# Experts stage of a hybrid encoder step: late dense tokens take the gates as stationary operand, and a piece's sum is kept in its PSUM bank by ScalarE and TensorE

## Chip, cores and metric

One core of one Trainium2 chip. The metric is the device time of one launch in microseconds. Every number below is in microseconds unless marked otherwise.

## The reference, cut to what matters

One layer of a streaming encoder for 1024 prompt tokens and 8 x 16 sample tokens (T = 1152 tokens, D = 1024 features) is computed in fp32. Its last part is a product-key expert layer: each token picks 8 x 16 of 128 x 128 experts, and every expert is one row of u and one row of v.

```python
w = jax.nn.softmax(fv, axis=-1)
act = jax.nn.gelu(jnp.einsum("thkd,td->thk", u[eidx], tb).astype(jnp.float32))
return jnp.einsum("thk,thkd->td", (w * act).astype(tb.dtype), v[eidx])
...
x = x + gate2 * peer_ffn(h2, peer_wq, peer_keys, peer_u, peer_v)
```

After that comes the final RMSNorm.

## The kernel before

Stages run one after the other: projections, a state-space scan, attention, branches, picks and gates, and from 2888.9 us to about 4825 us the experts stage (`phase_experts`), then `finish_output`. The diff touches the last two and the allocation of one array.

**Two ways to do the experts at once.** The first TD = 640 tokens ("dense") go through all 16,384 experts on TensorE, with the gates of the picked experts in a dense table and zeros elsewhere. The other 512 tokens (ST = 4 tiles of 128, "sparse") gather only their picked rows of u and v by indirect DMA, 128 rows of 4 KB (512 KB) at a time; VectorE forms the dot products and adds the weighted rows.

**Batches.** There are 64 batches of E = 2 blocks of 128 experts for the dense tokens, and two picks for each of the four sparse tiles. Each batch loads 2 x 512 KB of u, 2 x 512 KB of v, half of a 1280 KB slice of gates, and gathers 16 x 512 KB.

**Dense work of batch b.** fp32 products are made of three fp32r products (hi by hi, hi by lo, lo by hi), so every array is rounded by ScalarE (`round_u`, `round_v`, `round_g`) and its rest is formed by VectorE (`rest_of_u`, `rest_of_v`, `rest_of_g`). TensorE runs ahead with the u products of batch b+1 (L2290: 8 slices x 3 x 2 halves of 320 tokens, for each of 2 blocks = 96 matmuls of 320 columns into `ps`); ScalarE applies gelu into `act_` (L2365), VectorE multiplies by the gates (L2440), and the v products of batch b follow. Those are 8 output blocks d of 128 features, 6 matmuls each over 640 tokens:

- `keep(d)` for d = 0 to 3: v is stationary, and the sums stay in PSUM over all 64 batches, 512 tokens in `kept` (L2302, 24 matmuls of 512 columns in a batch) and 128 tokens in `kept_late` (L2301, 24 matmuls of 128 columns).
- `piece(b, j)` for j = 0 to 7 (SUMS = 8) does d = 4 to 7 in halves of 320 tokens into the one bank `pv` (L2310, 48 matmuls of 320 columns). Before each piece TensorE waits for `sum_r`: VectorE must have added the piece before it to `acc` in SBUF (`add_sums`, L2453). There is no second buffer.

```python
pe.wait_ge(sum_r, b * SUMS + j + START)
...
dve.wait_ge(sum_mm, b * SUMS + j + 1 + START)
v.tensor_tensor(acc[:, j // 2, a:a + HW], acc[:, j // 2, a:a + HW], pv[:, 0:HW], ALU.add).then_inc(sum_r, 1)
```

**Order.** The instruction order of each engine is written out by hand in a function `batch`. TensorE: the u products of block 0 of batch b+1 (48 matmuls), a wait for `v_lo` and `g_lo`, then `keep`, `piece` and two slices of block 1's u products in turn. ScalarE: `round_v` twice (each waits until all pieces of b-1 are done), `round_g`, then for m = 0 to 7 `weigh(b, m)` (gelu of a dot product and its share, two tiny instructions L2381 and L2383) with gelu and the rounding of u and g between them. VectorE: `rest_of_v`, `apply_gate`, `rest_of_v`, `rest_of_g`, then `dots(b, m)` (L2459), `add_rows(b, m)` (L2467) and the eight `add_sums` mixed. `add_rows(b, m)` needs `weigh(b, m)`, which needs `dots(b, m)`.

**Queues.** SP issues the loads of u, v and gates, each when the buffer is free (`u_lo`, `v_lo`, `gated`); u is loaded up to three batches ahead. GpSimd issues the gathers in the order u row 0, v row 0, u row 1, ... into four slots for u and four for v; each waits until VectorE has read the slot (`dot_r`, `row_r`).

**Finish.** ScalarE copies the kept sums to SBUF (L2424, L2425). `finish_output` takes the eight feature blocks in turn: x plus gated sums for the dense tokens (L2563), TensorE transposes the four sparse tiles (L2595), VectorE adds these, then squares, norm and store.

## Time and profile before

| | us |
|---|---|
| median of 3 runs (4875.52 to 4882.52) | 4880.63 |
| profiled execution, its own time | 4877.16 |
| span of its trace | 4875.0 |
| TensorE / VectorE / ScalarE / GpSimd busy, of the span | 4501.8 / 3520.9 / 1814.5 / 1519.1 |
| mean granted share of TensorE's clock | 0.961 |

Spans of instructions overlap where an engine is pipelined, so an engine's time for one instruction is read from the starts of two neighbours, not from the duration. DMA share is what the packets took, as a share of the 16 DMA engines' time; it can pass 1 a little.

### The profile page before, as it was taken

To read this page: it belongs to the slowest core of one execution; us is meant where nothing else is said; L and a number is where in the kernel's file an instruction comes from. 1 tells how busy PE (TensorE), PEld (TensorE's weight loads), DVE (VectorE), ACT (ScalarE), POOL (GpSimd) and SP (SyncE) were. 2 spreads that over 40 slices of the span, in tenths; PEclk is the share of its full clock that TensorE was granted. 3 is DMA by queue.
4 is the path that set the end of the run, shared out by engine and by line. 5 is a ranking of instruction groups with operands and counts; after the bars stand their busy time and mean duration, and the time that the engine had idled before them with its cause. 6 is when DMAs were issued, how large, how long until landed. Compare 5 with 4: busy or idle time off the path is not lost. (4 is left out here: it accounts for less than half of the span.)

```text
span 4875.0 us, 82654 instructions
## 1 busy us (share of the span) xinstructions
PE 4501.8 (92%) x28695; PEld 4177.5 (86%) x28695; DVE 3520.9 (72%) x6718; ACT 1814.5 (37%) x3800; POOL 1519.1 (31%) x1358
## 2 busy tenths in 40 slices
PE   7999999799989899969885779999999999999996
PEld 5999999799976598968874669999999999999995
DVE  3101555476754323447999979999999999999998
ACT  3111333244435531234444963333333333333332
POOL 0000000011210000000000017777777777777773
PEclk8999999899988899989997999999999999999998
DMA  4332222344433244338995569999999999999996
GB/s 164 107 137 96 87 89 84 129 141 142 138 115 62 68 161 168 140 124 306 352 329 199 207 235 367 359 378 372 371 370 375 375 370 362 372 380 377 377 371 247
DMA packets 351143, 1170.28 MB, mean 240 GB/s; under 512 B 40160, under 2 KB 91808, under 8 KB 344608
## 3 DMA queue, kind: packets, MB, share of 16 engines
q0 software_dynamic: 147456, 536.94, 29.3%
q1 hardware_dynamic: 160544, 483.06, 27.7%
q10 hardware_dynamic: 43008, 148.53, 8.1%
q8 instruction: 78, 1.28, 0.1%
q14 instruction: 57, 0.47, 0.0%
HBM read 971.20 MB, written 197.46 MB: 240 GB/s over the span
## 5 line engine op out<-in xcount | busy, mean ns | idle before, releaser
L2280 POOL DMA_INDIRECT ex_vr<-in_expert_v,ex_at x512 | 637.8, 1246 | 231.8 <-issue 154.3
L2278 POOL DMA_INDIRECT ex_ur<-scr_u_rows,ex_at x512 | 569.5, 1112 | 277.2 <-issue 118.1
L2467 DVE SCALAR_TENSOR_TENSOR ex_acc_rows<-ex_vr,ex_wt,ex_acc_rows 128x1024 f32<-128x1024 f32 x512 | 648.9, 1277 | 1.0 <-DMA ex_vr<-in_expert_v,ex_at 0.3
L2459 DVE SCALAR_TENSOR_TENSOR ex_ur<-ex_ur,h_rows 128x1024 f32<-128x1024 f32 x512 | 616.0, 1217 | 32.0 <-DMA ex_ur<-scr_u_rows,ex_at 30.8
L2272 POOL COPY ex_at<-picked_at 128x4 uint32 x128 | 96.5, 754 | 1465.5 <-POOLq L125 1465.0
L990 POOL TENSOR_TENSOR sd_cts<-sd_cT,sd_ea 128x512 f32<-128x512 f32 x72 | 98.6, 1369 | 1261.2 <-ACT sd_ea L880 1261.2
L2290 PE MATMUL ex_ps<-hd_hi,ex_u_hi 128*128 128x320 f32 x2048 | 469.5, 310 | 19.9 <-PEq L125 16.4
L2290 PE MATMUL ex_ps<-hd_lo,ex_u_hi 128*128 128x320 f32 x2048 | 469.3, 311 | 0.0
L2290 PE MATMUL ex_ps<-hd_hi,ex_u_lo 128*128 128x320 f32 x2048 | 468.5, 310 | 0.0
L2381 ACT ACTIVATE ex_gel<-ex_dot 128x1 f32<-128x1 f32 x512 | 103.7, 203 | 897.4 <-DVE ex_ur L2459 897.3
L479 DVE TENSOR_TENSOR pr_w_lo<-pr_w,pr_w_hi 128x1024 fp32r<-128x1024 f32 x56 | 68.6, 1226 | 487.8 <-ACT pr_w_hi L475 487.8
L2290 PEld LDWEIGHTS ex_ps<-hd_hi,ex_u_hi 128*128 128x128 f32 x2048 | 343.6, 189 | 20.6 <-issue 17.7
L2310 PE MATMUL ex_pv<-ex_g_hi,ex_v_hi 128*128 128x320 f32 x1024 | 329.1, 321 | 21.3 <-DVE ex_acc L2453 20.7
L2290 PEld LDWEIGHTS ex_ps<-hd_lo,ex_u_hi 128*128 128x128 f32 x2048 | 344.8, 189 | 0.0
L2290 PEld LDWEIGHTS ex_ps<-hd_hi,ex_u_lo 128*128 128x128 f32 x2048 | 344.1, 189 | 0.0
L331 PE MATMUL pr_ps<-h_hi,pr_w_hi 128*128 128x384 f32 x1392 | 320.7, 338 | 13.1 <-DVE h_lo L304 9.9
L331 PE MATMUL pr_ps<-h_lo,pr_w_hi 128*128 128x384 f32 x1392 | 317.8, 336 | 0.0
L331 PE MATMUL pr_ps<-h_hi,pr_w_lo 128*128 128x384 f32 x1392 | 317.6, 335 | 0.0
L2310 PE MATMUL ex_pv<-ex_g_lo,ex_v_hi 128*128 128x320 f32 x1024 | 316.8, 309 | 0.0
L2310 PE MATMUL ex_pv<-ex_g_hi,ex_v_lo 128*128 128x320 f32 x1024 | 315.3, 308 | 0.0
L331 PEld LDWEIGHTS pr_ps<-h_hi,pr_w_hi 128*128 128x128 f32 x1392 | 248.1, 189 | 18.7 <-issue 15.0
L331 PEld LDWEIGHTS pr_ps<-h_lo,pr_w_hi 128*128 128x128 f32 x1392 | 249.7, 189 | 0.0
(363 smaller groups left out, 11130.1 us busy)
## 6 DMA issues: line engine op xcount, KB each, us to landing
pk_raw_u<-in_expert_u SPq DMA_DIRECT2D x128, 512.0 KB, 6.5
scr_u_rows<-pk_rows_u ACTq DMA_DIRECT2D x128, 512.0 KB, 6.2
ex_u<-in_expert_u SPq DMA_DIRECT2D x128, 512.0 KB, 6.7
ex_v<-in_expert_v SPq DMA_DIRECT2D x128, 512.0 KB, 8.2
scr_gate<-gt_stage SPq DMA_DIRECT2D x10, 4096.0 KB, 12.6
ex_gate<-scr_gate SPq DMA_DIRECT2D x32, 1280.0 KB, 8.8
pr_w<-in_w_main SPq DMA_DIRECT2D x58, 512.0 KB, 4.6
scr_xbc<-pr_out ACTq DMA_DIRECT2D x32, 576.0 KB, 3.8
```

The costliest lines, as they stand in the source:

```text
L331: last = nc.tensor.matmul(ps[:, c, 0:CW], w[a][:, k], x[b][:, k, c * CW:(c + 1) * CW], start=(k == 0 and (a, b) == SPLIT[0]), stop=(k == k ...
L479: nc.vector.tensor_tensor(w2[1][:, s], w[:, s], w2[0][:, s].bitcast(F32), ALU.subtract).then_inc(w_lo[s], 1)
L990: nc.gpsimd.tensor_tensor(cts[:, q], cT[:, s, at].unsqueeze(1).to_broadcast([P, R, P]), ea[:, q], ALU.mult).then_inc(cts_r[q], 1)
L2272: nc.gpsimd.tensor_copy(at_now[:, h], at[:, :, ds(b * 2 + h, 1)].rearrange("p s j -> p (s j)")).then_inc(now_r, 1)
L2278: nc.gpsimd.indirect_dma_start(out=ur[:, s], out_offset=None, in_=scr["u_rows"], in_offset=by).then_inc(ur_in[s], 16)
L2280: nc.gpsimd.indirect_dma_start(out=vr[:, s], out_offset=None, in_=io["expert_v"].rearrange("j i d -> (j i) d"), in_offset=by).then_inc(vr_ ...
L2290: last = nc.tensor.matmul(ps[:, c, 0:HW], u2[x][:, e, k], hd[y][:, k, c * HW:(c + 1) * HW], start=(k == 0 and (x, y) == SPLIT[0]), stop=(k ...
L2310: last = nc.tensor.matmul(pv[:, 0:HW], v2[x][:, e, d * P:(d + 1) * P], g2[y][:, r, e, c * HW:(c + 1) * HW], start=(e == 0 and (x, y) == SP ...
L2381: nc.scalar.activation(gel[:, m:m + 1], dot[:, m:m + 1], ACT.Gelu_apprx_tanh).then_inc(gel_r, 1)
L2459: v.scalar_tensor_tensor(out=ur[:, s], in0=ur[:, s], scalar=1.0, in1=rows[:, s], op0=ALU.mult, op1=ALU.mult, accum_out=dot[:, m:m + 1]).th ...
L2467: v.scalar_tensor_tensor(out=acc_g[:, s], in0=vr[:, s], scalar=wt[:, m:m + 1], in1=acc_g[:, s], op0=ALU.mult, op1=ALU.add).then_inc(row_r[ ...
```

## The change

1. **Late dense tokens turned.** For tokens 512 to 639 the 128 gates (`g2[..., WIDE:TD]`) become the stationary operand and 512 columns of v the moving one (`late_tokens`). The result has tokens on partitions and features on columns: two halves of 512 features, 6 matmuls each. `kept_late` goes away.
2. **Wide pieces.** d = 4 to 7 now take 512 tokens in one piece (`wide_tokens`). With the two late halves there are SUMS = 6 pieces of 6 matmuls of 512 columns. `kept` is made with the same function.
3. **Sums in the bank.** `pv` has two banks. Before piece j ScalarE copies `sums[:, j]` from SBUF into bank j % 2 (`give_sums`, semaphore `given`), TensorE adds the piece on it (start=False), and ScalarE copies the bank back (`take_sums`). VectorE's `add_sums` goes away. Give j waits for take j-2. In ScalarE's order, take 5 of the batch before and give 1 stand ahead of `round_v`; take 0 and give 2 after `gelu(b+1, 0)`; take 1 and give 3 after weigh 3; take 2 and give 4 after weigh 4; take 3 and give 5 after weigh 5; take 4 and the next batch's give 0 before weigh 7.
4. **TensorE's order.** After the wait for v and g: for d = 0 to 3 `kept` d, piece d and two u slices; then pieces 4 and 5 (the late halves).
5. **Finish.** One copy for the kept sums. The sparse and the late dense tokens are transposed together: five transposes for a block in place of four; the first add spans 512 tokens in place of 640, the second 512 in place of 384.
6. `ex_acc` grows from 4 x 640 to 6 x 512 columns, and its view `picks` is written flat.

```diff
-                def keep(d, r, first, last):
+                def wide_tokens(out, d, r, first, last):
...
-                            w = v2[x][:, e, d * P:(d + 1) * P]
-                            begins, ends = first and e == 0 and (x, y) == SPLIT[0], last and e == E - 1 and (x, y) == SPLIT[-1]
-                            nc.tensor.matmul(kept_late[:, d], w, g2[y][:, r, e, WIDE:TD], start=begins and d == 0, stop=ends and d == KEPT - 1, skip_group_check=True)
-                            nc.tensor.matmul(kept[:, d], w, g2[y][:, r, e, 0:WIDE], start=begins, stop=ends, skip_group_check=True)
...
+                            mm = nc.tensor.matmul(out, v2[x][:, e, d * P:(d + 1) * P], g2[y][:, r, e, 0:WIDE],
...
+                def late_tokens(out, half, r, first, last):
...
+                            mm = nc.tensor.matmul(out, g2[y][:, r, e, WIDE:TD], v2[x][:, e, half * WIDE:(half + 1) * WIDE],
...
+                    pe.wait_ge(given, b * SUMS + j + 1 + START)
+                    if j < KD - KEPT:
+                        last = wide_tokens(pv[:, j % 2], KEPT + j, r, False, True)
+                    else:
+                        last = late_tokens(pv[:, j % 2], j - (KD - KEPT), r, False, True)
...
+                    for d in range(KEPT):
+                        wide_tokens(kept[:, d], d, r, first, last)
+                        piece(b, d, r)
+                        u_products(2 * d, 2 * d + 1)
+                    for j in range(KD - KEPT, SUMS):
+                        piece(b, j, r)
...
+                def give_sums(b, j, first=False):
+
+                    if not first:
+                        act.wait_ge(sum_r, b * SUMS + j - 1 + START)
+                    nc.scalar.copy(pv[:, j % 2], sums[:, j]).then_inc(given, 1)
+
+                def take_sums(b, j):
+                    act.wait_ge(sum_mm, b * SUMS + j + 1 + START)
+                    nc.scalar.copy(sums[:, j], pv[:, j % 2]).then_inc(sum_r, 1)
...
-                def add_sums(b, j):
-                    a = (j % 2) * HW
-                    dve.wait_ge(sum_mm, b * SUMS + j + 1 + START)
-                    v.tensor_tensor(acc[:, j // 2, a:a + HW], acc[:, j // 2, a:a + HW], pv[:, 0:HW], ALU.add).then_inc(sum_r, 1)
...
+                nc.tensor.transpose(pst[:, k % 2, 0:P], late_sums[half][:, at:at + P], ident)
```

## Rows read from the trace of the kernel before

**Rows 1.** Stretches of the experts stage: columns in the first line.

```profile
core 0: us, PE busy (x) PEld busy (x) DVE busy (x) ACT busy (x) POOL busy (x), PEclk, DMA share, GB/s
3000.00:4000.00 1000.00, 988.88 (x6410) 945.88 (x6409) 985.54 (x1336) 347.47 (x802) 740.94 (x666) 1.00 0.97 372
3487.50:3507.50 20.00, 20.00 (x131) 19.10 (x130) 19.61 (x28) 6.78 (x18) 15.17 (x14) 1.00 1.02 413
4780.00:4800.00 20.00, 14.88 (x96) 14.08 (x95) 18.48 (x26) 6.03 (x13) 15.75 (x15) 0.97 0.92 323
4800.00:4810.00 10.00, 9.34 (x41) 7.85 (x40) 9.63 (x15) 1.99 (x8) 6.30 (x6) 0.71 0.77 252
```

**Rows 2.** Line L2376: count, durations, first and last start.

```profile
L2376 ACT CAST ex_v_hi<-ex_v x128: 1037/1049/1058, 2908.4 to 4795.4; 128x1024 fp32r<-128x1024 f32 x128
```

**Rows 3.** DMA transfers from 3000 to 4500 us.

```profile
DMA packets 147747, 557.68 MB, mean 372 GB/s; under 512 B 16417, under 2 KB 16417, under 8 KB 144545
```

**Rows 4.** Waits, 3000 to 4500 us: total us, times, longest.

```profile
PEld ex_pv L2310 <- DVE ex_acc L2453: 26.3, 36, 4.3
DVE ex_ur L2459 <- DMA ex_ur<-scr_u_rows,ex_at: 18.3, 20, 4.4
PE ex_pv L2310 <- DVE ex_acc L2453: 15.3, 17, 4.0
```

**Rows 5.** TensorE in order of time, block 0's u products and the first kept matmuls.

```profile
3512.22 0.46 PE L2290 MATMUL ex_ps<-hd_hi,ex_u_hi 128*128 128x320 f32 x2
...
3516.33 0.46 PE L2290 MATMUL ex_ps<-hd_hi,ex_u_lo 128*128 128x320 f32 x2
3516.62 0.22 PE L2301 MATMUL ex_kept_late<-ex_g_hi,ex_v_hi 128*128 128x128 f32 x1
3516.68 0.45 PE L2302 MATMUL ex_kept<-ex_g_hi,ex_v_hi 128*128 128x512 f32 x1
3516.96 0.22 PE L2301 MATMUL ex_kept_late<-ex_g_lo,ex_v_hi 128*128 128x128 f32 x1
```

**Rows 6.** TensorE in the queries stage, in order of time.

```profile
2239.90 0.40 PE L1841 MATMUL pk_ps<-hg_hi,pk_w_hi 128*128 128x512 f32 x1
2240.13 0.46 PE L1840 MATMUL pk_ps<-hd_lo,pk_w_hi 128*128 128x320 f32 x2
```

**Rows 7.** VectorE in order of time, around one batch's end.

```profile
3510.80 0.48 DVE L2453 TENSOR_TENSOR ex_acc<-ex_acc,ex_pv 128x320 f32<-128x320 f32 x1
3511.20 1.22 DVE L2448 TENSOR_TENSOR ex_v_lo<-ex_v,ex_v_hi 128x1024 fp32r<-128x1024 f32 x1
...
3514.20 0.82 DVE L2444 TENSOR_TENSOR ex_g_lo<-ex_act,ex_g_hi 128x640 fp32r<-128x640 f32 x1
3514.94 1.22 DVE L2459 SCALAR_TENSOR_TENSOR ex_ur<-ex_ur,h_rows 128x1024 f32<-128x1024 f32 x1
```

**Rows 8.** GpSimd's gathers by line, 3000 to 4500 us.

```profile
L2280 POOL DMA_INDIRECT ex_vr<-in_expert_v,ex_at x400 | 499.8, 1250 | 168.3 <-issue 120.1 <-DVE ex_acc_rows L2467 48.3
L2278 POOL DMA_INDIRECT ex_ur<-scr_u_rows,ex_at x401 | 447.9, 1117 | 216.4 <-issue 91.7 <-DVE ex_ur L2459 65.0 <-POOL ex_share L2273 59.7
```

**Rows 9.** ScalarE in order of time, around the same batch's end.

```profile
3509.86 2.00 ACT L2376 CAST ex_v_hi<-ex_v 128x1024 fp32r<-128x1024 f32 x2 [2.01 <-PE ex_pv L2310]
...
3516.20 0.20 ACT L2381 ACTIVATE ex_gel<-ex_dot 128x1 f32<-128x1 f32 x1 [2.29 <-DVE ex_ur L2459]
3516.43 0.29 ACT L2383 ACTIVATE ex_wt<-ex_gel,ex_share 128x1 f32<-128x1 f32 x1
```

**Rows 10.** Line L1317: ScalarE copies 512 columns out of PSUM.

```profile
L1317 ACT COPY at_pT<-at_psT x68: 570/587/594, 1475.7 to 1683.0; 128x512 f32<-128x512 f32 x64, 16x512 f32<-16x512 f32 x4
```

**Rows 11.** ScalarE after the last batch.

```profile
4822.13 1.87 ACT L2424 COPY h_rows<-ex_kept 128x2048 f32<-128x2048 f32 x1 [2.27 <-PE ex_pv L2310]
4823.89 0.59 ACT L2425 COPY h_rows<-ex_kept_late 128x512 f32<-128x512 f32 x1
```

More of the change, by code:

```diff
@@ L2419, in _ @@
                 batch(BATCHES - 1, 1, False, False)
-                act.wait_ge(sum_mm, BATCHES * SUMS + START)
+                take_sums(BATCHES - 1, 5)
+                act.wait_ge(sum_r, BATCHES * SUMS + START)
                 for s in range(ST):
                     act.wait_ge(dot_r[s], BATCHES * 2 + START)
-                nc.scalar.copy(early[:, :, 0:WIDE], kept[:])
-                nc.scalar.copy(early[:, :, WIDE:TD], kept_late[:]).then_inc(early_r, 1)
+                nc.scalar.copy(early, kept[:]).then_inc(early_r, 1)
             @block.vector
@@ L2481, in batch @@
                         dots(b, 2)
-                    add_sums(b, 0)
                     if not dots_ahead:
@@ L2485, in batch @@
                     add_rows(b, 2)
-                    add_sums(b, 1)
                     add_rows(b, 3)
@@ L2500, in batch @@
                     add_rows(b, 5)
-                    add_sums(b, 5)
                     dots(b, 6)
@@ L2504, in batch @@
                     add_rows(b, 6)
-                    add_sums(b, 6)
                     if more:
@@ L2529, in _, with finish_output @@
                 dve.wait_ge(early_r, 1 + START)
-        finish_output(nc, io, per, scr, [early[:, k] for k in range(KEPT)] + [acc[:, k] for k in range(KD - KEPT)], acc_g, x_first, x_in, fg)
-def finish_output(nc, io, per, scr, acc, acc_g, x_first, x_in, fg):
-    LP = SEQ - TD
+        finish_output(nc, io, per, scr, [early[:, k] for k in range(KEPT)] + [sums[:, k] for k in range(KD - KEPT)], (sums[:, KD - KEPT], sums[:, KD - KEPT + 1]), acc_g, x_first, x_in, fg)
+def finish_output(nc, io, per, scr, acc, late_sums, acc_g, x_first, x_in, fg):
+    WIDE = TD - P
+    LP = SEQ - WIDE
     with ExitStack() as ctx:
@@ L2593, in turn @@
                     pe.wait_ge(x_r, k - 1 + START)
+                half, at = k // (KD // 2), k % (KD // 2) * P
+                nc.tensor.transpose(pst[:, k % 2, 0:P], late_sums[half][:, at:at + P], ident)
                 for s in range(ST):
-                    last = nc.tensor.transpose(pst[:, k % 2, s * P:(s + 1) * P], acc_g[:, s, k * P:(k + 1) * P], ident)
+                    last = nc.tensor.transpose(pst[:, k % 2, (s + 1) * P:(s + 2) * P], acc_g[:, s, k * P:(k + 1) * P], ident)
                 last.then_inc(turned, 1)
```

71 lines of the change are left out of this document (34 added, 37 removed).

## Prediction

> **What bounds the kernel now.** I read the page by slices first, to find the stage: from about 2890 us on all engines and the DMA are near full, so this stage is a period that repeats 64 times, and everything below is per batch. The period comes from the first and last rounding of v [rows 2]: 126 roundings lie between the first and the one before the last, which starts 0.95 before the last (two take 2.00 together, each 1.05 [rows 9]). (4794.4 - 2908.4) / 63 = 29.94 us.
>
> Then each resource, by the stretch table [rows 1] and the starts of neighbours:
>
> - VectorE: busy 985.5 of 1000, which is 29.5 of 29.94.
> - TensorE: matmuls of 320 columns start every 0.147 (28 of them from 3512.22 to 3516.33 [rows 5]); a pair of 128 and 512 columns takes 0.34 (3516.62 to 3516.96 [rows 5]). 96 + 48 of the first and 24 pairs: 21.2 + 8.2 = 29.4. It idles only for `add_sums`: 26.3 as its weight loads show it, over the 50.1 batches in 1500 us (1500 / 29.94), is 0.5 [rows 4].
> - GpSimd: busy 741 of 1000 is 22.2. Its idle time ahead of the gathers that is not a wait for VectorE is (120.1 + 91.7 + 59.7) / 50.1 = 5.4, so it has 27.6 of its own; another 113.3 / 50.1 = 2.3 is waiting for VectorE to free a slot [rows 8].
> - DMA: 557.68 MB in 1500 us is 11.13 MB a batch [rows 3]. Its share is 0.97 at 372 GB/s, and this looks full. But a stretch of 20 us moved 413 GB/s at a share of 1.02 [rows 1]. At 413 a batch needs 27.0.
> - ScalarE: busy 347 of 1000, 10.4.
>
> VectorE waits for gathers only 18.3 / 50.1 = 0.4 a batch [rows 4], and GpSimd waits for VectorE. So VectorE sets the period, TensorE stands 0.1 behind it, and the two touch in the single bank `pv`. Taking load off only one of them would give next to nothing. This change takes load off both.
>
> **The change, part by part.**
>
> *VectorE* loses 8 `add_sums`. One is 0.40 from start to start (3510.80 to 3511.20 [rows 7]), so 3.2, and 29.5 - 3.2 = 26.3 remain.
>
> *TensorE* has the same 61,440 columns, but 156 matmuls in place of 192. 96 u products stay at 14.1. 60 matmuls of 512 columns replace the rest. Their price: in the pairs of before, one takes 0.28 until the next start (3516.68 to 3516.96 [rows 5]), with the weights of a 128-column matmul to be swapped just behind; in the queries stage one takes 0.23 until a 320-column one starts (2239.90 to 2240.13 [rows 6]). Now each is followed by another long matmul, so I take 0.23: 13.8, sum 27.9, 1.5 less than before. At 0.28 it would be 16.8, sum 30.9; the short matmul, which I hold responsible for it, is gone.
>
> *ScalarE* gains 6 gives and 6 takes of 512 columns. A copy of 512 columns out of PSUM takes 0.59 [rows 10]. No row shows ScalarE writing PSUM from SBUF; below, a copy of 1024 columns from SBUF to SBUF at 1.05 [rows 2] gives an upper bound of 1.05 for half as many, and 0.59 is the nearest for the lower; I take 0.6. 12 x 0.6 = 7.2, together 17.6 of 28: hidden as a sum. What matters is order. The Trainium skill (ScalarE: Activation LUTs, "Step-by-step: what each stage is for") says that PSUM is the faster destination for ScalarE; no row here shows it, and it would leave 0.6 or less.
>
> *The batch's end* is where the copies lie on a path. Before: ScalarE starts `round_v` at 3509.86, when the last piece is done [rows 9]; VectorE finishes `rest_of_g` at 3514.94 [rows 7]; TensorE, busy with 48 u products, needs it at 3516.62 [rows 5]: 1.7 to spare. Now take 4 is released when piece 4 ends, 6 x 0.23 = 1.4 before the end: 3508.5. Take 0.6, give 0.6 (it waits for the take to complete): 3509.7. Weigh 7, two tiny instructions, 0.2 and 0.3 [rows 9]: 3510.2. Take 5 and give 1: 3511.4. So `round_v` starts 1.5 later than before, VectorE's four instructions follow as before, and 0.2 of the 1.7 is left. The edge is free, but only just. Queued behind these copies are `round_v`, `round_g` and the next weighs, for which VectorE's `rest_of_v` and `add_rows` 7 wait: `add_rows` 7 can end 1.2 after weigh 7, at 3511.4, and the first v rounding ends at 3512.4, so VectorE gets a hole of 1.0 here out of its new slack of 27.9 - 26.3 = 1.6.
>
> *Inside the batch* pieces 2, 3, 4, 5 need gives that stand behind weighs. A take and its give end 1.2 after the piece. From the end of piece 3 to the start of piece 5 TensorE has two u slices (12 x 0.147 = 1.8) and piece 4 (1.4): give 5 has 3.2 - 1.2 = 2.0 to spare. From piece 2 to piece 4 it has two times two u slices, a kept block and a piece, 6.4: give 4 has 5.2. Gives 2 and 3 have a kept block more, 6.6. The weighs wait for `dots`, so a late gather now delays a give, and a give later than these margins stops TensorE. Before, only the roundings were exposed so.
>
> *GpSimd and DMA* issue the same work. VectorE frees slots sooner, so the 2.3 that GpSimd waits shrinks; its floor is 27.6, if a gather's issue costs what it does now.
>
> *Finish and last batch.* The last batch loses its 8 `add_sums`, -3.2 (VectorE sets it). The last take lies ahead of the kept copy, +0.6; the copy of `kept_late`, 0.59 [rows 11], goes. One more transpose in each of eight turns, at about the spacing of a matmul, +1.2. The two adds of a block swap 128 columns between them, nothing. The first two gives run while ScalarE has no work. Together -2.
>
> **The sum.** Floors are now TensorE 27.9, GpSimd 27.6, DMA 27.0, VectorE 26.3. Before, the period was 0.4 above the highest floor (29.5). Now three floors lie within 1 us, the edge has 0.2 to spare, and at 27.9 the DMA would have to run at 97% of its best stretch (27.0 / 27.9); I take twice that loss, 0.8 (a choice): 28.7. 63 x (29.94 - 28.7) = 78. Span 4875.0 - 78 - 2 = 4795. The profiled execution was 2.2 above its span, and the median of the runs is 3.5 above that execution: 4801.
>
> At one place the skill speaks against any gain. The Trainium skill (DMA: Bandwidth & Descriptors, "Where 436 GB/s comes from") says that transfers between HBM and SBUF are bound by the HBM's share of a core, about 358 GB/s, and not by the fabric's 435. By that a batch would need 31.1, more than it takes; the trace disagrees with 372 over 1500 us and 413 over 20 [rows 1, 3].
>
> **Rivals.**
>
> 1. *The DMA is full already.* The share of 0.97 is real, and 413 GB/s is a favourable stretch, not a rate to be had over a batch. Then the most is 372 / 0.97 = 383 GB/s, 29.0 a batch, and with the loss of before 29.4: 63 x 0.54 = 34, time 4845. For it: the share. Against: shares over 1 at 413, and VectorE hardly waits for data. Chance 0.20. In its harder form the mean of 372 is the limit, and the period stays: 4878, no change, 0.05.
> 2. *The copies' round trip stops TensorE* (slower). Place: take 4, give 0, weigh 7, take 5, give 1 at the batch's end. It decides once each of the four copies costs about 0.4 more than 0.6: the chain is 1.6 longer, 0.2 of it hidden, so 1.4 goes on 28.7: 30.1, time 4889. For it: the price of a write into PSUM isn't in the trace, its upper bound is 1.05, and weigh 7 can hang on a gather. Against: reads cost 0.59. Chance 0.06.
> 3. *TensorE's clock.* The granted clock is 1.00 in the steady stretch, but 0.97 and 0.71 in the last batches, where TensorE had gaps [rows 1]. If the new waits bring a mean of 0.95, TensorE needs 29.4, and with 0.4 the period is 29.8: 4867. Chance 0.06.
> 4. *All losses go.* Two banks and a VectorE with slack absorb the jitter, period 28.0: 63 x 1.94 = 122, time 4757. Chance 0.08.
>
> **The numbers.** My forecast has 0.55, its own range from a period of 28.3 to one of 29.2: 4776 to 4832. The range for 8 in 10 reaches to rival 4 below and past the middle of rival 1 above: 4757 to 4857. About 0.2% (10 us) is what a measurement of this kernel can tell from no change. Faster: 0.55 + 0.20 + 0.08 + most of rival 3, 0.87; same: the hard form of rival 1 and the rest, 0.06; slower: rival 2 and something unseen, 0.07.
>
> **What would show it.** `ex_v_hi` from first to last over 63 should give 28.7. Neighbouring 512-column matmuls should be 0.23 apart. VectorE should fall to about 92% busy in the stage and wait for ScalarE's v roundings at the batch's end. ScalarE should be near 60% busy, gives and takes at 0.6 each. The DMA should move about 388 GB/s. If it moves 380 and VectorE waits for gathers by microseconds in a batch, rival 1 is right. If TensorE waits for `given` or `v_lo` by more than 1 us a batch, rival 2. The forecast fails if 512-column matmuls keep 0.28, or if GpSimd's issues become longer as the DMA fills.

## The result and the profile after

The changed kernel takes 4917.43 us (median of 6 runs, 4909.38 to 4924.16), the kernel before 4881.58 (6 runs beside them): ratio 1.0074, 95% interval 1.0061 to 1.0086. I had forecast 4801, 1.6% faster; it became 0.7% slower, outside the range.

The profiled execution took 4910.8, its span is 4909.0, 34.0 longer than before. The page's busy times and the line of the v roundings:

```profile
PE 4439.5 (90%) x26399; PEld 3992.7 (81%) x26399; DVE 3334.7 (68%) x6206; ACT 2234.6 (46%) x4567; POOL 1603.8 (33%) x1358
```

```profile
L2374 ACT CAST ex_v_hi<-ex_v x128: 1038/1047/1056, 2912.9 to 4828.9; 128x1024 fp32r<-128x1024 f32 x128
```

By the same working as for [rows 2], a batch takes (4828.9 - 1.0 - 2912.9) / 63 = 30.40; it was 29.94 and should have been 28.7. That is 63 x 0.46 = 29 of the 34 us. The first rounding starts 4.5 later, behind code that is the same; over all kernels told of here this start lies anywhere from 2900.9 to 2928.2, so I read nothing into it. The end takes the last 0.5. So the change of the period is all there is to explain.

The stretches, which answer to [rows 1]:

```profile
core 0: us, PE busy (x) PEld busy (x) DVE busy (x) ACT busy (x) POOL busy (x), PEclk, DMA share, GB/s
3000.00:4000.00 1000.00, 937.66 (x5139) 833.27 (x5138) 875.01 (x1051) 557.67 (x1181) 773.70 (x658) 1.00 0.97 367
```

VectorE went from 985.5 busy to 875.0, TensorE from 988.9 to 937.7. In a batch VectorE works 0.875 x 30.40 = 26.6. The load did leave both engines, and the period grew. Only GpSimd became busier with work that nobody changed, 740.9 to 773.7.

Who waits (total us, times, longest), 3000 to 4500 us, where there are 1500 / 30.40 = 49.3 batches; compare [rows 4]:

```profile
DVE ex_ur L2478 <- DMA ex_ur<-scr_u_rows,ex_at: 166.3, 97, 4.7
...
PE ex_kept L2300 <- DVE ex_g_lo L2468: 57.0, 43, 2.8
...
PE ex_ps L2291 <- ACT ex_act L2363: 30.1, 56, 1.1
DVE ex_v_lo L2472 <- ACT ex_v_hi L2374: 15.8, 21, 1.0
...
PE ex_pv L2308 <- ACT ex_pv L2387: 5.2, 7, 1.8
DVE ex_acc_rows L2486 <- DMA ex_vr<-in_expert_v,ex_at: 5.5, 18, 0.5
```

The first row is the new stall: VectorE waits for gathered rows for (166.3 + 5.5) / 49.3 = 3.5 a batch; before it was 0.4. The 3.2 that `add_sums` gave back turned into this wait. 97 waits are two a batch, and the timeline puts them at `dots` 3 (1.85 on a mean of 50 batches) and `dots` 7 (1.32). `dots` 7 stands shortly ahead of `rest_of_v` and `rest_of_g`, and so TensorE waits for `g_lo` as well, 57.0 / 49.3 = 1.2 a batch. The wait for the gives (last but one) is 0.1.

GpSimd by line, which answers to [rows 8] (count, busy and mean ns, idle before and what ended it):

```profile
L2281 POOL DMA_INDIRECT ex_vr<-in_expert_v,ex_at x394 | 507.9, 1289 | 158.9 <-issue 119.9 <-DVE ex_acc_rows L2486 39.0
L2279 POOL DMA_INDIRECT ex_ur<-scr_u_rows,ex_at x395 | 494.5, 1252 | 185.1 <-issue 90.5 <-POOL ex_share L2274 83.2 <-DVE ex_ur L2478 11.4
```

The issue of one gather takes 1.27 on the mean of both lines; before it took 1.18. By the working of the prediction GpSimd now has (1155.83 + 119.9 + 90.5 + 83.2 + 0.4) / 49.3 = 29.4 of its own in a batch (1155.83 is its busy time from 3000 to 4500). The prediction had 27.6. Of the 1.8 more, 16 x 0.09 = 1.4 is the longer issue; most of the rest is the gap behind the two small copies, part of which was counted as a wait for VectorE before.

GpSimd in order of time, half a batch before and half after the two copies of indices and shares:

```profile
3545.27 0.96 POOL L2279 DMA_INDIRECT ex_ur<-scr_u_rows,ex_at  x1 [0.90 <-POOL ex_share L2274]
3546.53 0.94 POOL L2281 DMA_INDIRECT ex_vr<-in_expert_v,ex_at  x1 [0.30 <-issue]
...
3550.86 0.93 POOL L2279 DMA_INDIRECT ex_ur<-scr_u_rows,ex_at  x1 [0.30 <-issue]
3552.09 1.97 POOL L2281 DMA_INDIRECT ex_vr<-in_expert_v,ex_at  x1 [0.30 <-issue]
3554.37 1.56 POOL L2279 DMA_INDIRECT ex_ur<-scr_u_rows,ex_at  x1 [0.30 <-issue]
3556.24 1.56 POOL L2281 DMA_INDIRECT ex_vr<-in_expert_v,ex_at  x1 [0.30 <-issue]
3557.80 0.38 POOL L2273 COPY ex_at<-picked_at 128x4 uint32 x1
3558.13 1.26 POOL L2274 COPY ex_share<-picked_share 128x4 f32 x1
3560.29 1.08 POOL L2279 DMA_INDIRECT ex_ur<-scr_u_rows,ex_at  x1 [0.90 <-POOL ex_share L2274]
3561.68 0.94 POOL L2281 DMA_INDIRECT ex_vr<-in_expert_v,ex_at  x1 [0.31 <-issue]
3562.92 0.94 POOL L2279 DMA_INDIRECT ex_ur<-scr_u_rows,ex_at  x1 [0.30 <-issue]
3564.17 0.94 POOL L2281 DMA_INDIRECT ex_vr<-in_expert_v,ex_at  x1 [0.30 <-issue]
3565.41 1.79 POOL L2279 DMA_INDIRECT ex_ur<-scr_u_rows,ex_at  x1 [0.31 <-issue]
```

and VectorE in the same stretch:

```profile
3552.03 1.21 DVE L2472 TENSOR_TENSOR ex_v_lo<-ex_v,ex_v_hi 128x1024 fp32r<-128x1024 f32 x1
3553.17 0.81 DVE L2464 TENSOR_TENSOR ex_act<-ex_act,ex_gate 128x640 f32<-128x640 f32 x1
3553.91 1.21 DVE L2472 TENSOR_TENSOR ex_v_lo<-ex_v,ex_v_hi 128x1024 fp32r<-128x1024 f32 x1
...
3561.60 0.07 DVE L2478 DVE_READ_ACCUMULATOR ex_ur<-ex_ur,h_rows 128x1 f32 x1
3565.17 1.23 DVE L2478 SCALAR_TENSOR_TENSOR ex_ur<-ex_ur,h_rows 128x1024 f32<-128x1024 f32 x1 [3.49 <-DMA ex_ur<-scr_u_rows,ex_at]
```

Three things are to be seen. GpSimd pauses only for its 0.3 between issues and the 0.9 behind the copies. While VectorE stands still (3561.7 to 3565.2) three gathers take 0.94 each; of those shown that start under its instructions four take 1.56 to 1.97, and two do not (0.93 at 3550.86 and 1.08 at 3560.29, both within an `add_rows`). From 3000 to 4600 us it is the same: the 144 gathers that start while VectorE stands still take 0.94, none over 0.97; of the 695 others 307 take over 1.5 and 231 under 1.0. And the row that `dots` 3 waits for at 3565.17 is that of the issue at 3554.37: 10.8 from issue to use. From that, two theories and their rivals.

- **GATHERS**: a gather's issue is lengthened by what VectorE does, and the `add_sums` had been gaps. Of 855 gathers before (3000 to 4600 us), the 203 that start within an `add_sums` take 0.938 on the mean; of the 652 others 353 take 1.1 to 1.7, 67 more, and 232 less. GpSimd thereby comes close to its limit.
- **LOOP**: GpSimd issues in one fixed order into few slots, and that closes a circle: `add_rows` 2 frees a slot, then follow the issues v6, u7, v7, the copies, u0, v0, u1, v1, u2, v2, u3, then the landing, `dots` 3, `add_rows` 2. Once round is one batch, so its pieces, from each start to the next, add up to the period whatever the limit is (17.2 + 10.4 + 2.4 = 30.0 before, 17.8 + 10.2 + 2.4 = 30.5 after), and their sum shows nothing. What tells is the slack: how long the row of u3 has lain there when `dots` 3 starts. By the landings in the trace it is 1.35 on the mean of 50 batches before, and under 0.3 in 14 of them; after, it is 0.22 on the mean of 49, and under 0.3 in 44. So the circle is closed at this joint in nine of ten batches of the changed kernel, and was open in most of the kernel before. [rows 4] says the same: 20 waits for such rows in 50 batches, against 97 in 49.
- **EDGE** (rival): the copies ahead of `round_v` delay the batch's end.
- **DMA FULL** (rival 1 of the prediction): the share of 0.97 is a limit.

### The profile page after: what moved, and what is told of

Its sections match the earlier page's. It is cut to its first block and busy times, and to the rows that moved or that the text cites. A ratio compares the mean times of both kernels' runs of the same rounds, so it can differ in the third digit from the quotient of the medians.

```text
span 4909.0 us, 78618 instructions
## 1 busy us (share of the span) xinstructions
PE 4439.5 (90%) x26399; PEld 3992.7 (81%) x26399; DVE 3334.7 (68%) x6206; ACT 2234.6 (46%) x4567; POOL 1603.8 (33%) x1358
## 3 DMA queue, kind: packets, MB, share of 16 engines
q0 software_dynamic: 147456, 536.94, 29.2%
q1 hardware_dynamic: 160544, 483.06, 27.7%
## 5 line engine op out<-in xcount | busy, mean ns | idle before, releaser
L2281 POOL DMA_INDIRECT ex_vr<-in_expert_v,ex_at x512 | 656.8, 1283 | 216.7 <-issue 156.1
L2279 POOL DMA_INDIRECT ex_ur<-scr_u_rows,ex_at x512 | 643.5, 1257 | 238.9 <-issue 118.1
L2273 POOL COPY ex_at<-picked_at 128x4 uint32 x128 | 67.6, 528 | 1466.0 <-POOLq L125 1465.5
L2300 PE MATMUL ex_kept<-ex_g_hi,ex_v_hi 128*128 128x512 f32 x512 | 205.8, 402 | 77.8 <-DVE ex_g_lo L2468 77.7
L2391 ACT COPY ex_acc<-ex_pv 128x512 f32<-128x512 f32 x384 | 221.8, 578 | 66.6 <-PE ex_pv L2300 62.6
L331 PEld LDWEIGHTS pr_ps<-h_hi,pr_w_lo 128*128 128x128 f32 x1392 | 249.3, 189 | 0.0
```

Of the source, the lines that this page charges most:

```text
L331: last = nc.tensor.matmul(ps[:, c, 0:CW], w[a][:, k], x[b][:, k, c * CW:(c + 1) * CW], start=(k == 0 and (a, b) == SPLIT[0]), stop=(k == k ...
L2273: nc.gpsimd.tensor_copy(at_now[:, h], at[:, :, ds(b * 2 + h, 1)].rearrange("p s j -> p (s j)")).then_inc(now_r, 1)
L2279: nc.gpsimd.indirect_dma_start(out=ur[:, s], out_offset=None, in_=scr["u_rows"], in_offset=by).then_inc(ur_in[s], 16)
L2281: nc.gpsimd.indirect_dma_start(out=vr[:, s], out_offset=None, in_=io["expert_v"].rearrange("j i d -> (j i) d"), in_offset=by).then_inc(vr_ ...
L2300: mm = nc.tensor.matmul(out, v2[x][:, e, d * P:(d + 1) * P], g2[y][:, r, e, 0:WIDE], start=first and e == 0 and (x, y) == SPLIT[0], stop=l ...
L2391: nc.scalar.copy(sums[:, j], pv[:, j % 2]).then_inc(sum_r, 1)
```

## The experiments

Ratios are to the kernel before, each beside its own runs. "Own" is GpSimd's busy time, issue gaps and gaps behind the copies, in a batch; "V waits" is VectorE waiting for gathers, "G waits" GpSimd waiting for VectorE, both in a batch; all from 3000 to 4500 us. Period and waits are those of the one profiled execution, which for round_first was 23 above the median in the second column, for one_copy 18 and for one_copy_half_gathers 9, and for best_memsets 11 below it (10 us are 0.16 of a period); all others lie within 8.

| kernel | us | ratio (95%) | period | issue | own | V waits | G waits |
|---|---|---|---|---|---|---|---|
| before | 4881.58 | 1 | 29.94 | 1.18 | 27.6 | 0.4 | 2.3 |
| changed | 4917.43 | 1.0074 (1.0061-1.0086) | 30.40 | 1.27 | 29.4 | 3.5 | 1.0 |
| round_first | 4918.96 | 1.0079 (1.0062-1.0096) | 30.75 | 1.28 | 29.5 | 4.0 | 1.2 |
| one_copy | 4920.06 | 1.0082 (1.0065-1.0099) | 30.62 | 1.28 | 27.0 | 3.1 | 3.6 |
| small_loads | 4895.39 | 1.0037 (1.0023-1.0051) | 30.23 | 1.33 | 29.8 | 3.1 | 0.4 |
| before_one_copy | 4869.39 | 0.9985 (0.9973-0.9996) | 29.84 | 1.14 | 25.2 | 0.2 | 4.7 |
| u_ahead | 4933.27 | 1.0116 (1.0093-1.0140) | 30.91 | 1.33 | 30.2 | 3.7 | 0.7 |
| u_ahead_one_copy | 4887.12 | 1.0015 (1.0003-1.0027) | 30.00 | 1.32 | 27.8 | 2.3 | 2.2 |
| one_copy_small_loads | 4856.73 | 0.9959 (0.9941-0.9976) | 29.61 | 1.31 | 27.6 | 2.2 | 2.0 |
| vector_adds | 4893.23 | 1.0027 (1.0014-1.0041) | 30.14 | 1.22 | 27.4 | 0.2 | 2.7 |
| vector_memsets | 4867.04 | 0.9969 (0.9954-0.9985) | 29.75 | 1.14 | 27.1 | 0.6 | 2.7 |
| before_scalar_copies | 4925.33 | 1.0075 (1.0050-1.0099) | 30.66 | 1.19 | 27.7 | 0.2 | 2.9 |
| one_copy_half_gathers | 4818.10 | 0.9859 (0.9837-0.9880) | 28.87 | 1.35 | 28.3 | 0.8 | 0.5 |
| best_try | 4870.79 | 0.9976 (0.9963-0.9989) | 29.79 | 1.35 | 27.0 | 2.1 | 2.8 |
| before_tiny_adds | 4874.71 | 0.9992 (0.9976-1.0008) | 29.84 | 1.17 | 27.6 | 1.3 | 2.3 |
| best_memsets | 4843.67 | 0.9933 (0.9917-0.9950) | 29.39 | 1.22 | 25.9 | 0.3 | 3.5 |

The circle in the kernels that issue the gathers in the same order, means over the batches that start between 3000 and 4500 us: (a) from the end of `add_rows` 2 to the start of u3's issue, (b) from there to the landing of its row, (c) `dots` 3 and `add_rows` 2. The circle without its slack is a + b + c; "period" is that of the same batches; the last column has the slack and how many batches have less than 0.3 of it.

| kernel | a | b | c | a + b + c | period | slack at `dots` 3 |
|---|---|---|---|---|---|---|
| before | 17.2 | 9.0 | 2.4 | 28.6 | 29.96 | 1.35, 14 of 50 |
| changed | 17.8 | 10.0 | 2.4 | 30.2 | 30.47 | 0.22, 44 of 49 |
| one_copy | 17.8 | 10.3 | 2.4 | 30.6 | 30.58 | 0.02, 49 of 49 |
| small_loads | 19.3 | 8.0 | 2.4 | 29.7 | 30.26 | 0.58, 26 of 50 |
| vector_adds | 16.6 | 8.7 | 2.4 | 27.7 | 30.12 | 2.44, 6 of 50 |
| vector_memsets | 16.7 | 9.1 | 2.4 | 28.2 | 29.78 | 1.64, 10 of 51 |
| one_copy_half_gathers | 19.3 | 6.7 | 2.4 | 28.5 | 28.85 | 0.38, 30 of 52 |
| before_tiny_adds | 17.1 | 9.7 | 2.4 | 29.2 | 29.88 | 0.65, 31 of 50 |

### First: which of the theories

**round_first.** In the changed kernel ScalarE rounds v ahead of take 5 and give 1.

```diff
-                    if reused:
-                        take_sums(b - 1, 5)
-                        give_sums(b, 1)
                     round_v(b, 0)
                     round_v(b, 1)
+                    if reused:
+                        take_sums(b - 1, 5)
+                        give_sums(b, 1)
```

> The changed kernel, but ScalarE rounds v for a batch before it takes the last sum of the batch before and gives the second, so that the two copies (0.6 us each) no longer lie ahead of the roundings. Theory EDGE (the copies at the batch's end hold up TensorE, which waits about 2 us a batch there): the period falls by up to 1.2 from 30.4 us, 63 x 1.2 = 75, about 4840. Theory GATHERS (GpSimd issues the gathers one after the other almost without a pause, and VectorE has to stop for them): no change, within 0.3% of the changed kernel. Theory DMA (the DMA engines are full): no change.

TensorE's wait for `g_lo` fell from 57.0 to 35.6, as it should; the time did not move. EDGE falls: what it takes from one wait comes back in another.

**one_copy.** The two small copies on GpSimd, made for each half of a batch, are made once for the whole batch: 2 instead of 4.

```diff
-                        nc.gpsimd.tensor_copy(at_now[:, h], at[:, :, ds(b * 2 + h, 1)].rearrange("p s j -> p (s j)")).then_inc(now_r, 1)
-                        nc.gpsimd.tensor_copy(share_now[:, h], share[:, :, ds(b * 2 + h, 1)].rearrange("p s j -> p (s j)")).then_inc(now_r, 1)
+                        nc.gpsimd.tensor_copy(at_now[:, q], at[:, :, ds(g * 4 + q * 2, 2)]).then_inc(now_r, 1)
+                        nc.gpsimd.tensor_copy(share_now[:, q], share[:, :, ds(g * 4 + q * 2, 2)]).then_inc(now_r, 1)
```

> The changed kernel, but GpSimd copies the indices and shares of a whole batch at once (two copies a batch in place of four, into buffers that change with the batch). Theory GATHERS: GpSimd's own time falls by half of its copies, about 0.5 + 1.1 + 0.9 = 2.5 us a batch, and the period by 1 to 2: 4790 to 4855. Theory EDGE and theory DMA: no change, within 0.3%.

GpSimd's own time fell by 2.4 to 27.0, and the time stayed. So a full GpSimd alone isn't the cause, and the expectation of GATHERS missed. The waits show what holds it:

```profile
POOL ex_vr L2283 <- DVE ex_acc_rows L2488: 158.5, 92, 4.8
DVE ex_ur L2480 <- DMA ex_ur<-scr_u_rows,ex_at: 145.6, 65, 5.0
```

In one and the same batch GpSimd waits 3.6 for VectorE and VectorE 3.1 for GpSimd's gathers. No engine is full (VectorE 26.6, GpSimd 27.0), and the period is 30.6: two engines that wait for each other in turn are a circle. It is closed at both joints: v6 waits for `add_rows` 2 in 46 of 49 batches, and the row of u3 lands just ahead of `dots` 3 in all 49. The pair of copies that stayed lies between v7 and u0, on that circle; the pair that went did not.

**small_loads.** The loads of u and v for the dense tokens bring an eighth of each block (the rest of the buffers keeps old data, so the dense part computes on it).

```diff
-                        sp.dma_start(u[:, e], io["expert_u"][ds(b * E + e, 1)].rearrange("e p k c -> p (e k) c")).then_inc(u_in[e], 16)
+                        sp.dma_start(u[:, e, 0:1], io["expert_u"][ds(b * E + e, 1), :, 0:1].rearrange("e p k c -> p (e k) c")).then_inc(u_in[e], 16)
```

> The changed kernel, but after the first batches only 128 of 1024 columns of the dense u and v blocks are loaded (the other columns keep what an earlier batch left, which is left out of the computation), with the same number of issues: 9.3 MB a batch in place of 11.1. Theory DMA: the period falls with the bytes, by 2 to 5 us a batch, 130 to 300 in all: 4610 to 4790. Theory GATHERS: the gathers are issued as before; at most they land earlier, 0 to 1 a batch: 4850 to 4917. Theory EDGE: no change.

From 3000 to 4500 us:

```profile
3000.00:4500.00 1500.00, 1410.25 (x7725) 1248.77 (x7726) 1318.80 (x1590) 842.07 (x1785) 1180.12 (x991) 1.00 0.88 308
```

With 308 GB/s and a share of 0.88 the kernel is only 0.4% faster than the changed one and still slower than before. DMA FULL falls for this kernel: with a sixth fewer bytes a batch should have become 2 to 5 shorter, and became 0.2 shorter (0.35 by the medians). The load of the DMA does count in another way, as the row of u3 now lands 8.0 after the start of its issue in place of 10.0. Now it is GpSimd that is full: own 29.8 of 30.23.

**before_one_copy.** The edit of one_copy, in the kernel before.

> The kernel before with the same edit of GpSimd's copies (two a batch in place of four). If VectorE sets the period of the kernel before, as the prediction has it, no change: within 0.3% of 4881. If GpSimd set it there too, 1 us or more a batch is gained: 4820 or less.

0.15% faster, its interval just below 1, and within the 0.3% of the first forecast: GpSimd took 2.4 less a batch, waits for VectorE (now 4.7) in place of it, and had next to no share in the period there. The issues became a little shorter, 1.14.

### Second: the circle and GpSimd's fullness together

**u_ahead.** GpSimd issues u row s+1 ahead of v row s, so u3 comes one issue earlier on the circle (`u_row` and `v_row` hold the wait and the gather of a slot, unchanged).

```diff
+                        u_row(0)
                         for s in range(ST):
+                            if s + 1 < ST:
+                                u_row(s + 1)
+                            v_row(s)
```

> The changed kernel, but GpSimd issues each gather of u one place earlier: u0 u1 v0 u2 v1 u3 v2 v3 in place of u0 v0 u1 v1 u2 v2 u3 v3. In the changed kernel u3 starts 5.5 us after its slot is free, because it stands behind v2, and v2 waits for add_rows 6 of the batch before; VectorE then stops 1.9 us for u3 and 1.3 us for u7. Theory LOOP (add_rows 6, issue of v2, issue of u3, landing, dots 3, and on to the next add_rows 6 is a circle that sets the period): VectorE's stops shrink by about 2 us and the period by 1 to 2: 4790 to 4855. Theory ISSUE (GpSimd's issues are simply full, in any order): no change within 0.3% of 4917.

Slower, and LOOP's expectation missed: the wait moved from the u rows (38.9) to the v rows (138.4), the issues rose to 1.33, and GpSimd was full, 30.2 of 30.91. The order can do nothing where GpSimd has no time left.

**u_ahead_one_copy.** Both edits.

> The changed kernel with both: u one place earlier, and GpSimd's index and share copies once a batch. If the circle and GpSimd's own time are two limits close to one another, this is faster than either alone: LOOP expects a period of 28.3 to 29.2, 4780 to 4840. If neither is what sets the period: 4900 to 4925.

1.0015 against 1.0116 and 1.0082 for the edits alone: with time left on GpSimd the other order gains 33 us, 0.5 a batch by the medians (0.6 by the profiles). It is faster than either edit, as LOOP expects, but the size missed: 30.00 where LOOP had 28.3 to 29.2.

**one_copy_small_loads.** Both edits (it leaves out what small_loads leaves out).

> The changed kernel with GpSimd's copies once a batch and with 128 of 1024 columns of the dense u and v blocks loaded (the rest is left out). Each edit alone gave 0 and 22 us. Theory LOOP (landing time and issue time both lie on the circle, and each hid the other): together they give more than their sum, a period of 29.3 or less, 4850 or less. If they only add: about 4895.

Against the changed kernel one_copy gave nothing and small_loads 22 us; together they give 61 (4917.43 - 4856.73; by the ratios, which take out how the kernel before drifted, 18 and 56). That is more than the sum, as it must be where two limits lie side by side: GpSimd's own time (29.4) and the circle. one_copy lifts the first, faster landing the second. The forecast of 29.3 or less and 4850 was missed by 0.3 and 7 us.

**vector_adds.** Wide pieces and late tokens as in the change, but VectorE adds the sums as before, with 512 columns and two banks; ScalarE copies nothing.

```diff
-                    take_sums(b, 0)
-                    give_sums(b, 2)
...
+                def add_sums(b, j):
+                    dve.wait_ge(sum_mm, b * SUMS + j + 1 + START)
+                    v.tensor_tensor(sums[:, j], sums[:, j], pv[:, j % 2], ALU.add).then_inc(sum_r, 1)
```

> One part of the change alone: TensorE's new shapes (512 columns, late tokens turned) and two banks, but VectorE adds each finished piece to the sums as before, six adds of 512 columns, and ScalarE gives and takes nothing. VectorE then has 26.3 + 6 x 0.6 = 29.9 us a batch. Theory PORT (VectorE's instructions with one operand in PSUM let GpSimd through, those with two in SBUF hold its gathers up, so removing the adds cost GpSimd more than it gave VectorE): the mean gather falls back from 1.27 to about 1.18 us, period 29.5 to 30.0, 4855 to 4885. If the mean gather stays at 1.27: period 30.4 or more, 4917 or more.

VectorE is busy 1489.07 of 1500, and nobody waits for a gather any more (0.2). So the cause of the 3.5 lies in that half of the change which moves the sums from VectorE to ScalarE; this run does not part the adds from ScalarE's copies, the next two do. Six adds of 512 columns (0.674 each) cost VectorE more than eight of 320 (0.478): it is busy 29.9 a batch of 30.14, and sets the period. The theory's 1.18 and 29.5 to 30.0 were missed by a little on both.

### Third: what lengthens a gather's issue

**vector_memsets.** The changed kernel with work for nothing: at eight places of a batch VectorE clears a spare tile of 64 columns twice.

```diff
+                def pass_time(b, i):
+                    for n in range(2):
+                        dve.wait_ge(blank_r, b * 16 + i * 2 + n + START)
+                        v.memset(blank[:], 0.0).then_inc(blank_r, 1)
```

> The changed kernel, but where the eight adds stood VectorE now writes a small blank tile twice (64 columns, each waiting for the one before), about 0.4 us each time, 3.2 a batch: the time of the removed adds comes back, with no operand read from SBUF. Theory PORT with the circle: GpSimd's gathers get through in these gaps, their mean falls from 1.28 to about 1.2, and VectorE's stops for gathers (3.4 a batch) take up the added time: period 29.9 to 30.4, 4885 to 4917. If VectorE's own work sets the period of the changed kernel: 30.4 + 3.2 = 33.6, about 5120. If the circle holds and the port plays no part: no change, 4910 to 4925, and a gather mean of 1.28.

```profile
L2282 POOL DMA_INDIRECT ex_vr<-in_expert_v,ex_at x403 | 469.3, 1165 | 177.4 <-issue 123.0 <-DVE ex_acc_rows L2492 54.3
L2280 POOL DMA_INDIRECT ex_ur<-scr_u_rows,ex_at x403 | 448.7, 1113 | 225.7 <-issue 92.1 <-DVE ex_ur L2484 80.3 <-POOL ex_share L2275 53.4
```

More work for VectorE, and the kernel is 1.0% faster than the changed one (0.9969 / 1.0074) and 0.3% faster than before. The issues fell from 1.27 to 1.14, GpSimd's own time from 29.4 to 27.1, VectorE's wait from 3.5 to 0.6. Gathers over 1.5 us were 10% before, 37% in the changed kernel, 16% here. The slack at `dots` 3 is back at 1.6. This is the strongest support for GATHERS. The run does not say whether the memsets work as gaps in VectorE's access to SBUF, or by moving its instructions against the issues. Nor is it shown what now holds the kernel at 29.75: by busy time VectorE has 28.0 and TensorE 28.4, and the circle has 28.2.

**before_scalar_copies.** The kernel before, in which ScalarE also makes 18 copies of 288 columns a batch between two spare arrays.

```diff
+                def spare(b, i):
+                    for n in range(3):
+                        act.wait_ge(blank_r, b * 18 + i + n + START)
+                        nc.scalar.copy(blank[:, 1], blank[:, 0]).then_inc(blank_r, 1)
```

> The kernel before, with 18 spare ScalarE copies a batch (288 columns, SBUF to SBUF, about 0.45 us each) behind weighs 1 to 6: ScalarE becomes as busy as in the changed kernel, off every path but its own order. Theory PORT: VectorE's instructions are the same, so the gathers stay at a mean of 1.18 and the time within 0.3% of 4880. If ScalarE's load or its order is what lengthens the gathers or the period: a mean of 1.25 or more, and 4900 or more.

The issues stay at 1.19: ScalarE does not lengthen them. But the kernel is 0.75% slower, which I had not expected: VectorE waits for `u_hi` (27.0 in 1500 us) and TensorE for gelu (38.7). ScalarE's place in the order has a price of its own even at 57% busy. These copies stand right behind the weighs, other places than the takes and gives have, so the size does not carry over; but part of the loss in the changed kernel may be of this kind (there TensorE waits 30.1 for gelu).

**one_copy_half_gathers.** one_copy, in which each gather brings 512 columns of each row in place of 1024 (the other half stays zero).

```diff
-indirect_dma_start(out=ur[:, s], out_offset=None, in_=scr["u_rows"], in_offset=by)
+indirect_dma_start(out=ur[:, s, 0:512], out_offset=None, in_=scr["u_rows"].rearrange("r (t d) -> (r t) d", t=2), in_offset=by)
```

> The changed kernel with GpSimd's copies once a batch, and each gather moves 128 rows of 2 KB in place of 4 KB (the other half of each row stays at zero, and the rows read are others; this is left out of the computation). The issues are the same. Theory LOOP: the landing of u3 (10.3 us after its issue starts) lies on the circle, so the period falls until the next limit, TensorE's 28.0 or GpSimd's 27.5: 28.0 to 28.8, 4770 to 4820. If landing doesn't matter: 4905 to 4925.

```profile
L2284 POOL DMA_INDIRECT ex_vr<-in_expert_v,ex_at x416 | 587.5, 1412 | 151.5 <-issue 123.5 <-DVE ex_acc_rows L2489 27.9
L2282 POOL DMA_INDIRECT ex_ur<-scr_u_rows,ex_at x417 | 535.7, 1285 | 158.2 <-issue 111.2 <-POOL ex_share L2276 47.0
```

28.87, 1.75 less than one_copy (1.6 by the medians), with the same number of instructions on every engine: the row of u3 lands after 6.7 in place of 10.3, and the landing lies on the circle. Which part of the DMA's relief does it, the smaller gathers or the freer queues, one run does not say. The floor met next is GpSimd's: (1190.35 + 123.5 + 111.2 + 47.0) / 52.0 = 28.3 of 28.87, with issues of 1.35. TensorE and VectorE had room for the forecast period of 28.7; landing and issues had not.

**best_try.** u_ahead_one_copy, and the copy of the shares moves from GpSimd to ScalarE.

```diff
-                        nc.gpsimd.tensor_copy(share_now[:, q], share[:, :, ds(g * 4 + q * 2, 2)]).then_inc(now_r, 1)
+                    nc.scalar.copy(share_now[:, r], share[:, :, ds(b * 2, 2)]).then_inc(share_r, 1)
```

> The changed kernel with u one place earlier, one index copy a batch on GpSimd, and the shares copied by ScalarE, which is 60% busy, in place of GpSimd. GpSimd loses another 1.1 to 1.5 us a batch against the kernel with u ahead and one copy (4887, period 30.0). Theory LOOP: period 29.0 to 29.7, 4825 to 4870, ahead of the kernel before. If it stays at 4880 to 4890, GpSimd's copies are no longer on the circle, and VectorE's stops for v rows (2.0 a batch) come from the landing alone.

0.24% faster than before, at 29.79, a hair outside the forecast 4825 to 4870. GpSimd's own time fell by 0.8 against u_ahead_one_copy, of which 0.6 came back as waits for VectorE and 0.2 as a shorter period.

### Last: the kernel before, and both remedies together

**before_tiny_adds.** The kernel before with `add_sums` of 8 columns (the rest of the sums is left out), so VectorE has 2 us a batch less to do and all waits are as they were.

```diff
-v.tensor_tensor(acc[:, j // 2, a:a + HW], acc[:, j // 2, a:a + HW], pv[:, 0:HW], ALU.add)
+v.tensor_tensor(acc[:, j // 2, a:a + 8], acc[:, j // 2, a:a + 8], pv[:, 0:8], ALU.add)
```

> The kernel before, with the eight adds of VectorE cut to 8 of 320 columns (the rest of these sums is left out), so that nearly all of what the change takes from VectorE goes, and TensorE's shapes and ScalarE's work stay. By the prediction, VectorE's 29.5 falls to about 27 and TensorE's 29.4 becomes the floor: 29.4 to 29.8, 4847 to 4872. By the theory that VectorE's adds let GpSimd's gathers through and that the circle of gathers sets the period: gathers of a mean above 1.22, VectorE stops for them by 2 us or more a batch, and a period of 29.9 or more: 4880 to 4920. If it is 4880 or more, taking work from VectorE alone explains the loss.

Same time. VectorE's busy time falls to 1376.41 of 1500, and its wait for gathers rises from 0.4 to 1.3 a batch. So VectorE did not set the period by itself. TensorE fits: it is busy 1481.98 of 1500, 29.5 a batch of 29.84, and the prediction had it 0.1 behind VectorE. The circle came nearer (29.2, slack 0.65) but is closed in 31 of 50 batches only. Both forecasts missed, the first by 3 us; the second wanted issues above 1.22, and they stayed at 1.17 although an add now takes 0.155 in place of 0.478. So it is not the adds' time that lets gathers through; a short break seems to do, as with the memsets.

**best_memsets.** best_try and the memsets (44 columns wide).

> The changed kernel with u one place earlier, one index copy a batch on GpSimd, shares copied by ScalarE, and the sixteen blank writes of VectorE a batch (44 columns each). If the gaps for GpSimd and its smaller load add up, the period is 29.0 to 29.5, 4825 to 4855, the fastest of all. If both only ease the same circle down to VectorE's 29.6 of work and waits: 4860 to 4875.

4843.67, 0.7% faster than before and 1.4% faster than the changed kernel (0.9933 / 1.0074), the fastest here that leaves nothing out. VectorE waits only 0.3 a batch for gathers; at 29.39 no engine is full and the DMA moves 379 GB/s at a share of 0.99. That is the 29.4 which rival 1 of the prediction had for a full DMA, and no run rules that out for this kernel. The two remedies alone gave 0.61 (best_try) and 0.65 (vector_memsets) of the changed kernel's 30.40, together 1.01; by the medians 0.74, 0.80 and 1.17.

## Why the prediction was wrong

**The step that failed** is the list of floors in the sum: "Floors are now TensorE 27.9, GpSimd 27.6, DMA 27.0, VectorE 26.3". One of its terms was too small, and one floor was not in it.

*The term* is GpSimd's "27.6, if a gather's issue costs what it does now". The cost rose from 1.18 to 1.27, and GpSimd's own time to 29.4, above every floor in the list. The prediction named longer issues as what would break it, but for the wrong reason, a DMA that fills: the DMA moved less (367 against 372 GB/s), and in small_loads, with a lighter DMA, the issues were longer still (1.33). They depend on what VectorE does: vector_memsets (1.14) shows it, vector_adds (1.22) agrees, and before_scalar_copies (1.19) shows that ScalarE's load doesn't lengthen them.

*The missing floor* is a path that leads through several engines and ends where it began: GpSimd's issues in order, the landing, `dots`, `add_rows`, the slot. Each floor in the list was one engine's work divided by time, so this path could not be in it. Without its slack it takes 28.6 in the kernel before: more than any floor of the list, though still just under the 28.7 of the forecast. In the changed kernel it takes 30.2, and the period is 30.4. So what broke the forecast is that this path got longer. Of the 1.7 more, 0.9 is in the nine issues ahead of u3 (10.4 to 11.3), 0.5 in u3's own (1.06 to 1.52), and 0.5 in the rest of its landing (7.95 to 8.5), less 0.2 in the copies and pauses. Why the rest of the landing became longer is open.

That the circle holds the changed kernel is shown by one_copy (mutual waits, closed in every batch, GpSimd's own time down to 27.0 and nothing gained), by the pair one_copy and small_loads, and by one_copy_half_gathers. In the changed kernel itself GpSimd's own 29.4 lies close beside it: v6 waits for `add_rows` 2 in 13 of 49 batches, and in the others GpSimd comes later by itself. That the longer issues are what VectorE's missing adds cost is shown by vector_memsets, which puts breaks in their place and gets the 1.14, the slack of 1.6 and the time back. The changed kernel took 3.2 from VectorE and 1.5 from TensorE, neither of which lay on these limits, and both got it back as waits: 3.5 and 1.8 ((57.0 + 30.1) / 49.3).

"So VectorE sets the period, TensorE stands 0.1 behind it" is about the kernel before, and no run speaks against it: before_one_copy took 2.4 from GpSimd and before_tiny_adds 2.1 from VectorE, each for 0.1 a batch, and the row of u3 lay ready for 1.35. It told what held the kernel before. It did not tell what would hold the next one.

The Trainium skill (SBUF — State Buffer, "Who interferes with whom") says that a VectorE instruction with two inputs in SBUF contends with GpSimd's reads of SBUF, and one with at most one such input does not, outside the modes that take both ports. The `add_sums` had one input in PSUM, and issues that started in them took 0.938, which agrees; so does 0.937 for the 162 that started in a memset. But more than half of the 300 gathers of the changed kernel that start in an `add_rows`, which has two inputs in SBUF, take 0.94 too, so the rule alone does not price an issue. The page adds, as inferred, that `tensor_tensor` leaves the writing of descriptors alone; the gather of 1.97 that starts at 3552.09, with nothing but such instructions beside it, speaks against its being free.

**The other steps.**

- *TensorE's price*: right. Neighbours of 512 columns start 0.23 apart, not 0.28:

```profile
3531.04 0.39 PE L2300 MATMUL ex_kept<-ex_g_lo,ex_v_hi 128*128 128x512 f32 x1
3531.27 0.39 PE L2300 MATMUL ex_kept<-ex_g_hi,ex_v_lo 128*128 128x512 f32 x1
3531.50 0.39 PE L2300 MATMUL ex_kept<-ex_g_hi,ex_v_hi 128*128 128x512 f32 x1
```

- *VectorE's relief*: right, 26.6 against 26.3.
- *The copies*: 0.6 was right for both. The row of the gives (min/median/max ns):

```profile
L2387 ACT COPY ex_pv<-ex_acc x296: 590/591/595, 3001.2 to 4495.8; 128x512 f32<-128x512 f32 x148
```

  The takes have a median of 0.577. The Trainium skill (ScalarE: Activation LUTs, "Step-by-step: what each stage is for") has PSUM as the faster destination. Rows with the same source agree by a little: 512 columns out of SBUF take 0.591 into PSUM and 0.613 into SBUF (L1699 of the kernel before, a cast). The takes are shorter still, but their source is another.
- *The batch's end*: worked out well, and not decisive. ScalarE around one end:

```profile
3518.17 0.59 ACT L2387 COPY ex_pv<-ex_acc 128x512 f32<-128x512 f32 x1
...
3519.33 0.59 ACT L2391 COPY ex_acc<-ex_pv 128x512 f32<-128x512 f32 x1
3519.95 0.59 ACT L2387 COPY ex_pv<-ex_acc 128x512 f32<-128x512 f32 x1
3520.48 2.00 ACT L2374 CAST ex_v_hi<-ex_v 128x1024 fp32r<-128x1024 f32 x2
```

  VectorE's `rest_of_g` ends at 3525.39, TensorE's u products at 3525.60: 0.2 to spare, as predicted. Where TensorE does wait for `g_lo`, mostly a gather was late; round_first moved this wait and not the time.
- *Rival 1* (DMA full): its signs were "380 GB/s and VectorE waits for gathers by microseconds". The second came without the first. A wait for a landing is no sign that the DMA is full; it can have been issued late. small_loads refutes it for the changed kernel; at 29.39 (best_memsets) it may be met.
- *Rival 2* (round trip): the right direction, slower, by the wrong mechanism. Waits for gives are 0.1 a batch. But before_scalar_copies shows that ScalarE's extra work costs by its order, at other waits (gelu, `u_hi`); how much of the 0.46 is of that kind stays open.
- *Rival 3* (clock): the granted clock is 1.00 from 3000 to 4000 and 0.99 to 4500, so this rival falls.
- *The loss of 0.8*, a choice, had no source; the range was built from engines' floors and could not hold the outcome.

**Open**: how VectorE lengthens an issue, whether through the port or through the phase in which its instructions meet the issues; a run with memsets moves both. How the 0.46 divides between longer issues (shown to matter by vector_memsets) and ScalarE's order (shown only in the kernel before). And what holds vector_memsets at 29.75 and best_memsets at 29.39.

## What to carry to other kernels

Besides each engine's floor, add up every circle through buffers: from the instruction that frees a slot, through the issues queued ahead in the same queue, the landing and the users, back to that instruction. Measured from each start to the next, the pieces of such a circle always add up to the period, so look for its slack: how long each landed row lay ready before its use. Here it was 1.35. A gain larger than the slack comes back as waits, and so does whatever makes the path itself longer. Two engines that wait for each other in turn, with neither full, are its sign. And a light instruction on a full engine can be worth its time as a gap for another: price a removed instruction by what its neighbours do meanwhile too.
